# A down projection by seven products of eight, with its weight sums made in DRAM, in a transformer-block kernel on one core

## The chip, the core and the metric

The kernel runs on one core of a Trainium2 chip. Its engines are TensorE (PE, and PEld for its weight loads), VectorE (DVE), ScalarE (ACT), GpSimd (POOL) and SyncE (SP); SP and POOL issue the transfers, which all share 16 DMA engines. The metric is the device time of one execution in microseconds (us). 128x512 is 128 partitions by 512 fp32 elements.

## The reference, cut to what matters

```python
h = x + swa_mixer(rms_norm(x, attn_norm), ...)           # sliding-window attention, D_MODEL = 1024, SEQ = 1024
a = relu(rms_norm(h, mlp_norm) @ w_up)                   # 1024 -> 4096
h = h + (a * a) @ w_down                                 # 4096 -> 1024
h = rms_norm(h, final_norm)
# a second block of two layers follows: modulation vectors silu(c) @ w_mod (48 columns of 128), convolution, Fourier mixing,
# window attention; it isn't touched except that the 48 modulation rows are worked out in another place
```

## The kernel before

Activations are held transposed: features on partitions, the 1024 tokens along the free axis in two halves ("ti" 0 and 1, TN = 512). Every fp32 product is made of three matmuls (`mm3`): each operand is split into a high part (fp32r, cast by ACT) and a low part (the difference, made by DVE), and high x high, high x low and low x high are accumulated. So a 128x128 block of weights against 512 tokens costs PE three matmuls, and every operand costs ACT one copy and DVE one subtraction.

Each engine has a program written out in a fixed order; semaphores tie them. SP issues nearly all loads.

**Attention.** `mixed_attention` walks 16 steps k through a plan of slots, two slots a step (37 in all). Step k's scores are made in slots 2k and 2k+1, the exponentials in 2k+2. In slot 2k+3 DVE makes the denominators, then DVE normalises the even heads and POOL the odd ones (`divide`, L1115). PE transposes the normalised heads (L891, `turn`) in slots 2k+4 (tiles 0 and 1, even heads; the tile of odd heads as well where a step has two tiles only) and 2k+5 (tiles 2 and 3, odd heads, which need `divide`). PE's gaps between these are filled with the rest of the query projection and the output projection (`heads_pe`). POOL has nothing else to do here.

**Up projection.** Four of the 32 blocks of 128 hidden features are made directly. The other 28 go in 14 pairs by Strassen's scheme in Winograd's form over (2 halves of the features in) x (2 blocks out) x (2 halves of the tokens): seven products of 4 x 3 matmuls replace eight. The t-tiles (t1 to t4) are the sums of activations, the "forms" 0 to 6 of a pair are its weights or sums of weights: forms 0, 5 and 6 are plain, forms 1 to 4 sums. `form_sums` makes the sums on POOL (L1420 to L1428) from the pair's rows in `sraw`; ACT casts (`form_high`) and DVE subtracts (`form_low`) each form four products ahead (LEAD). The products accumulate in banks of PSUM; ACT copies a bank out between two products (`take`), DVE adds (`add_out`, L1861) and squares (L1866), and SP spills the hidden tile to DRAM.

**Down projection.** All plain: quarters of 8 hidden chunks, 24 units d of 48 matmuls and 16 jobs (`DOWN3`) of 24 matmuls, 1536 matmuls in all. Each unit loads 512 KB of weights and two rows of `mod_w`; DVE adds each result to `hm` (L1897, L1921), splits chunks (L1481) and weights (L168), and multiplies out the modulations (L1888, 96 of them, two a row of `mod_w`) between them.

Of the kernel before, what the change touches and what calls it, by code (L numbers as in the profile page):

```python
# [30 lines left out]
P = 128  # L31
# [16 lines left out]
STAGES = [("qkv", 10), ("wo", 8), ("mlp", 36), ("ein", 20), ("dft", 6), ("fw", 1), ("pw", 2),  # L48
# [6 lines left out]
UNITS = _n  # L55

# [43 lines left out]
def build(nc, t):  # L100
# [13 lines left out]
    with es:  # L114
# [451 lines left out]
        mH = [sb(f"mH{ti}", [KC, TN], A_R + 32 * ti * KB, F32R) for ti in range(2)]  # L566
        mL = [sb(f"mL{ti}", [KC, TN], A_R + (32 * ti + 16) * KB, F32R) for ti in range(2)]
# [164 lines left out]
        def mixed_attention(name, steps, X, pairs, t_tiles, chunks, heads, W, QH, QL, KH, KL, vzH, vzL, in1, sink_of, logits,  # L732
# [372 lines left out]
            def att_pool(pool):  # L1105
# [233 lines left out]
        def vec(ti):  # L1339
            return 1 if ti == 2 else 0  # L1340

        QUARTERS, MODS = 4, 3
        base = W0["mlp"]


        UP_DIRECT, PAIRS, FORMS, LEAD = 4, 14, 7, 4
        DOWN0, PRODUCTS = base + UP_DIRECT, PAIRS * FORMS
        V11, V21, V12, V22 = (lambda k: t1V[:, k, :]), (lambda k: t4V[:, k, :]), (lambda k: t3V[:, k, :]), (lambda k: t2V[:, k, :])
        t1V, t4V, t3V, t2V = (sb(f"t{n}V", [HALF, TN], A_R + at * KB) for n, at in ((1, 96), (4, 104), (3, 128), (2, 136)))
        t1L, t4L, t3L, t2L = (sb(f"t{n}L", [HALF, TN], A_R + at * KB, F32R) for n, at in ((1, 96), (4, 104), (3, 128), (2, 136)))  # L1350
        t1H, t4H, t3H, t2H = (sb(f"t{n}H", [HALF, TN], A_R + at * KB, F32R) for n, at in ((1, 112), (4, 120), (3, 144), (2, 152)))
        FORM_AT = [(A_WST + 12 * KB + 2 * KB * i, A_WST + 2 * KB * i) for i in range(6)] + \
                  [(A_R + 34 * KB, A_R + 32 * KB), (A_R + 38 * KB, A_R + 36 * KB)]
        formH = [sb(f"formH{i}", [TN], h, F32R) for i, (h, l) in enumerate(FORM_AT)]
        formL = [sb(f"formL{i}", [TN], l, F32R) for i, (h, l) in enumerate(FORM_AT)]
        formS = [sb(f"formS{i}", [TN], l) for i, (h, l) in enumerate(FORM_AT)]
        CHUNK_AT = [(48, 52), (0, 16), (4, 20), (40, 56), (44, 60), (8, 24), (12, 28), (32, 36)] + \
                   [(96 + 8 * i, 100 + 8 * i) for i in range(8)]
        chunkH = [sb(f"chunkH{i}", [SEQ], A_R + h * KB, F32R) for i, (h, l) in enumerate(CHUNK_AT)]
        chunkL = [sb(f"chunkL{i}", [SEQ], A_R + l * KB, F32R) for i, (h, l) in enumerate(CHUNK_AT)]  # L1360
        chunkR = [sb(f"chunkR{i}", [SEQ], A_R + l * KB) for i, (h, l) in enumerate(CHUNK_AT)]
        taken_out = sb("taken_out", [3, TN], RX)
        sraw = sb("sraw", [4, D], RX + 6 * KB)
        hid = sb("hid", [4, TN], RX + 22 * KB)
        mod_junk = sb("mod_junk", [D], RX, BF16)
# [1868 lines left out]
```

## Time and profile before

| | |
|---|---|
| median of 3 runs | 2095.6 us (2094.21 to 2097.47) |
| the profiled execution | 2095.91 us, of which the span of its trace is 2094.1 us (1.8 us lie around it) |
| PE busy | 96% of the span, 10014 matmuls |
| DVE, ACT, POOL busy | 65%, 39%, 15% |
| attention | about 100 to 300 us |
| up projection by products | about 389 to 656 us |
| down projection | about 656 to 1016 us |

Busy time of PE is read with care: matmuls overlap, so that the count of matmuls in a stretch tells more than the busy share.

### The profile page before, as it was taken

How to read it: one execution, taken by the hardware profiler on the slowest of the kernel's cores; microseconds unless marked ns; L12 is line 12 of the kernel's file. 1: busy time of each engine (PE TensorE's matmuls, PEld its weight loads, DVE VectorE, ACT ScalarE, POOL GpSimd, SP SyncE). 2: the span in 40 equal slices, each digit the busy share in tenths (PEclk: the TensorE clock that was granted, in tenths of full speed). 3: DMA queues.
4: the chain of work that ended last, by engine and by line, in shares of the span. 5: the costliest groups of instructions: out<-in, count | busy, mean ns of one | idle time of the engine just before them, and what ended most of it. 6: DMA issues, size and time to landing. Idle time of an engine off the chain costs nothing. (4 is left out here: it accounts for less than half of the span.)

```text
span 2094.1 us, 26033 instructions
## 1 busy us (share of the span) xinstructions
PE 2012.5 (96%) x10014; PEld 1658.0 (79%) x10014; DVE 1360.1 (65%) x2307; ACT 810.1 (39%) x1499; POOL 304.8 (15%) x262
## 2 busy tenths in 40 slices
PE   6999999999998999999999999989989999999997
PEld 4877787888887888888788888778877777888785
DVE  7278877655445877773689895774363456777644
ACT  4266544533334121213531232741242235555432
POOL 2023223222220000002400010000020012222200
PEclk9999999999999999999999999999999999999998
DMA  3202000423326555531231165234122211011212
GB/s 129 70 21 102 22 30 31 142 109 112 124 98 219 187 197 191 211 121 51 60 121 41 41 158 142 73 107 153 33 103 71 71 55 39 27 37 41 113 44 90
DMA packets 61562, 198.32 MB, mean 95 GB/s; under 512 B 7168, under 2 KB 11904, under 8 KB 60288
## 3 DMA queue, kind: packets, MB, share of 16 engines
q1 hardware_dynamic: 57408, 180.58, 24.9%
q0 software_dynamic: 1584, 7.29, 1.8%
q10 hardware_dynamic: 2448, 8.79, 1.1%
q8 instruction: 80, 1.31, 0.3%
q14 instruction: 42, 0.34, 0.1%
HBM read 152.64 MB, written 36.70 MB: 90 GB/s over the span
## 5 line engine op out<-in xcount | busy, mean ns | idle before, releaser
L173 PE MATMUL banks<-u2H,wH 128*128 128x512 f32 (+1 forms) x704 | 261.0, 371 | 4.6 <-POOL u2L L435 2.9
L174 PE MATMUL banks<-u2L,wH 128*128 128x512 f32 (+1 forms) x704 | 257.2, 365 | 0.0
L175 PE MATMUL banks<-u2H,wL 128*128 128x512 f32 (+1 forms) x704 | 256.9, 365 | 0.0
L163 ACT CAST wH<-raw 128x1024 fp32r<-128x1024 f32 x125 | 130.9, 1048 | 270.6 <-DMA raw<-in_wstream 268.5
L173 PE MATMUL banks<-chunkH,wH 128*128 128x512 f32 x512 | 201.4, 393 | 5.7 <-DVE chunkL L1481 5.6
L168 DVE TENSOR_TENSOR wL<-raw,wH 128x1024 fp32r<-128x1024 f32 x125 | 156.3, 1251 | 77.1 <-ACT wH L163 76.7
L174 PE MATMUL banks<-chunkL,wH 128*128 128x512 f32 x512 | 200.3, 391 | 0.0
L175 PE MATMUL banks<-chunkH,wL 128*128 128x512 f32 x512 | 200.1, 391 | 0.0
L1115 POOL TENSOR_SCALAR logits<-logits,stat 128x256 f32<-128x256 f32 (+3 forms) x96 | 121.2, 1275 | 341.0 <-DVE stat L990 341.0
L2205 DVE SCALAR_TENSOR_TENSOR conv_out<-conv_in,par,conv_out 128x1295 f32<-128x1295 f32 x108 | 162.7, 1566 | 0.6
L1888 DVE SCALAR_TENSOR_TENSOR mod_junk<-mod_w,cvec 128x1024 bf16<-128x1024 f32 x96 | 117.4, 1223 | 59.2 <-DMA mod_w<-in_mod_w 57.6
L173 PEld LDWEIGHTS banks<-u2H,wH 128*128 128x128 f32 x704 | 133.8, 190 | 27.7 <-issue 4.6
L175 PEld LDWEIGHTS banks<-u2H,wL 128*128 128x128 f32 x704 | 133.7, 190 | 21.3
L174 PEld LDWEIGHTS banks<-u2L,wH 128*128 128x128 f32 x704 | 133.9, 190 | 20.2 <-issue 0.2
L173 PEld LDWEIGHTS banks<-chunkH,wH 128*128 128x128 f32 x512 | 96.6, 189 | 27.8 <-DVE chunkL L1481 7.6
L175 PEld LDWEIGHTS banks<-chunkH,wL 128*128 128x128 f32 x512 | 96.7, 189 | 20.2
L174 PEld LDWEIGHTS banks<-chunkL,wH 128*128 128x128 f32 x512 | 96.7, 189 | 19.9 <-issue 0.2
L1084 ACT ACTIVATE logits<-logits,stat 128x256 f32<-128x256 f32 (+3 forms) x192 | 112.0, 586 | 0.0
L1452 DVE TENSOR_TENSOR formL<-sraw,formH 128x512 fp32r<-128x512 f32 x42 | 33.9, 808 | 98.1 <-ACT formH L1443 98.1
L173 PE MATMUL banks<-w2H,wH 128*128 128x512 f32 x208 | 88.3, 425 | 4.1 <-DVE wL L168 3.4
L174 PE MATMUL banks<-w2L,wH 128*128 128x512 f32 x208 | 83.0, 399 | 0.0
L175 PE MATMUL banks<-w2H,wL 128*128 128x512 f32 x208 | 82.7, 398 | 0.0
(387 smaller groups left out, 4717.9 us busy)
## 6 DMA issues: line engine op xcount, KB each, us to landing
raw<-in_wstream SPq DMA_DIRECT2D x125, 512.0 KB, 3.6
mod_w<-in_mod_w SPq DMA_DIRECT2D x48, 512.0 KB, 6.0
hidden_scratch<-hid SPq DMA_DIRECT2D x64, 256.0 KB, 2.0
chunkR<-hidden_scratch SPq DMA_DIRECT2D x32, 512.0 KB, 4.5
sraw<-in_sstream SPq DMA_DIRECT2D x28, 512.0 KB, 4.4
side_sum<-side_tap POOLq DMA_DIRECT2D x11, 647.5 KB, 5.8
gt<-gates_scratch SPq DMA_DIRECT2D x8, 640.0 KB, 3.9
h<-in_x SPq DMA_DIRECT2D x4, 1024.0 KB, 10.8
```

The costliest lines, as they stand in the source:

```text
L163: act.copy(wH[:, u % R, :], raw[:, u % R, :]).then_inc(weights_hi, 1)
L168: eng.tensor_tensor(wL[:, u % R, :], raw[:, u % R, :], wH[:, u % R, :].bitcast(F32), ALU.subtract)\
L173: first = pe.matmul(out, aH, bH, start=start, stop=False, skip_group_check=more)
L174: pe.matmul(out, aH, bL, start=False, stop=False, skip_group_check=more)
L175: return first, pe.matmul(out, aL, bH, start=False, stop=stop, skip_group_check=more)
L1084: m = act.activation(src, src, ACT.Exp, bias=stat[:, NEG, k % 3, hs:hs + 1], scale=0.125 / factor(steps[k]), accum_out=stat[:, SUM, k % 3, ...
L1115: m = pool.tensor_scalar(src, src, stat[:, SUM, k % 3, hs:hs + 1], None, ALU.mult)
L1452: dve.tensor_tensor(formL[form_slot(f)][:], form_source(f), formH[form_slot(f)][:].bitcast(F32), ALU.subtract)\
L1888: dve.scalar_tensor_tensor(mod_junk[:], mod_w[:, n % MODS, :], 1.0, cvec[:, v, :], ALU.mult, ALU.mult, accum_out=modv[:, n, v:v + 1]).then ...
L2205: dve.scalar_tensor_tensor(dst, src, w, dst, ALU.mult, ALU.add).then_inc(conv_step, 1)
```

## The change

- **Down projection.** 24 of the 32 hidden chunks, as 12 pairs kp (chunks kp and kp + 12), go by seven products. An output step handles two of the 8 output blocks and a span lo to hi of the pairs (`DOWN_WINDOWS`): 15 steps, whose spans are staggered so that at most five pairs are held at a time. Of each pair DVE makes four sums and seven low parts, ACT seven high parts (`prepare` says in which product's slot). DVE adds each product's bank to two or fewer tiles of `hm` (`down_add`) between one product and the next of the same bank. The last 8 chunks stay plain: the 16 jobs of `DOWN3`.
- **Weight sums.** `form_sums` and `sraw` go. The sums of all 29 steps (14 up, 15 down) are made in DRAM (`presum_step`): for each group of 4 steps, 1 MiB an array, four copies DRAM to DRAM and four accumulating transfers, in six parts, each part of which waits on POOL for the transfers of the part before. Two groups (lanes) take turns. The first 28 of the 48 parts are issued in the attention's slots 0 to 13, two a slot, after POOL's `divide`; the rest after POOL's work on the norm. SP then loads every form by itself (`form_load`, 256 KB or less) into a ring of ten.
- **Modulations.** 36 of the 48 rows are multiplied out during the up projection (three a pair), 12 during `DOWN3`.
- **Squares.** The squaring of the hidden tiles goes from DVE to ACT, as a ReLU and a square each.

The diff, cut to its core:

```diff
+DOWN_WINDOWS = [(0, 2), (0, 2), (0, 3), (0, 4), (2, 5), (2, 6), (3, 7), (4, 8), (5, 9), (6, 10), (7, 10), (8, 12),
+           (9, 12), (10, 12), (10, 12)]
...
-            def att_pool(pool):
+            def att_pool(pool, beside=None):
...
                 for i, slot in enumerate(plan):
                     if slot.sums:
                         divide(slot.k - 1)
...
+                    if beside:
+                        beside(pool, i)
...
+        def presum_step(pool, group, part):
+            lo, hi = PRESUM_GROUP * group, min(PRESUM_GROUP * group + PRESUM_GROUP, STEPS)
+            turn, count = presum[group % 2], 128 * (group // 2)
...
+            if part or group >= 2:
+                pool.wait_ge(turn, count + (PRESUM_DONE[part - 1] if part else 0))
+            if part == 0:
+                pool.dma_start(R1, A21).then_inc(turn, 16)
+                pool.dma_start(R3, A11).then_inc(turn, 16)
+            if part == 1:
+                pool.dma_start(R1, A22, accum_op=ALU.add, max_dma_last_dim=8192).then_inc(turn, 16)
+                pool.dma_start(R3, A21, accum_op=ALU.add, max_dma_last_dim=8192).then_inc(turn, 16)
+            if part == 2:
+                pool.dma_start(R2, R1).then_inc(turn, 16)
+            if part == 3:
+                pool.dma_start(R2, A11, accum_op=ALU.add, max_dma_last_dim=8192).then_inc(turn, 16)
+            if part == 4:
+                pool.dma_start(R4, R2).then_inc(turn, 16)
+            if part == 5:
+                pool.dma_start(R4, A12, accum_op=ALU.add, max_dma_last_dim=8192).then_inc(turn, 16)
+
+        GROUPS = (STEPS + PRESUM_GROUP - 1) // PRESUM_GROUP
+        PRESUMS = [(2 * pair + lane, part) for pair in range((GROUPS + 1) // 2) for part in range(PRESUM_STEPS)
+                   for lane in range(2) if 2 * pair + lane < GROUPS]
+        PRESUMS_BESIDE = 28
+
+        def presum_slot(pool, i):
+            for group, part in PRESUMS[2 * i:2 * i + 2] if 2 * i < PRESUMS_BESIDE else ():
+                presum_step(pool, group, part)
+
+        def form_load(sp, f):
+            n, i = divmod(f, FORMS)
...
+            elif f >= RING:
+                sp.wait_ge(forms_begun, f - RING + 2)
...
+            if i in SUMS:
+                group = n // PRESUM_GROUP
+                sp.wait_ge(presum[group % 2], 128 * (group // 2) + PRESUM_DONE[(1, 3, 5, 1)[SUMS[i]]])
+            source = sums_d[SUMS[i]][n] if i in SUMS else t["sblocks"][PLAIN[i]][n]
+            sp.dma_start(form(formR, f), source[:, 0:width(n)]).then_inc(form_loaded[f % 4], 16)
...
+        prepare(0, -1, 1, {0: (X11, X1), 1: (X2, X22), 2: (X3, X21), 3: (X4,)},
+                {0: (SUM1, SUM2, SUM3, SUM4), 1: (X11, X1), 2: (X2, X22, X3), 3: (X21, X4)})
+        prepare(1, -1, 5, {0: (X11, X1), 1: (X2, X22), 2: (X3, X21), 3: (X4,)},
+                {0: (SUM1, SUM2), 1: (SUM3, SUM4, X11), 2: (X1, X2), 3: (X22,), 4: (X3,), 5: (X21,), 6: (X4,)})
+        prepare(2, 0, 4, {1: (X11, X1), 2: (X2,), 3: (X22,), 4: (X3,), 5: (X21,), 6: (X4,)},
+                {0: (SUM1,), 1: (SUM2,), 2: (SUM3,), 3: (SUM4,), 4: (X11,), 5: (X1,), 6: (X2,), 7: (X22,), 8: (X3,), 9: (X21,), 10: (X4,)})
...
+        for n, kp in PREP.items():
+            prepare(kp, n, 2, {1: (X11, X1), 2: (X2, X22), 3: (X3, X21), 4: (X4,)},
+                    {0: (SUM1, SUM2), 1: (SUM3, SUM4), 2: (X11, X1), 3: (X2, X22), 4: (X3, X21), 5: (X4,)})
...
-            for q in range(PAIRS):
-                form_sums(pool, q)
-            pool.wait_ge(down_done, 48)
+            for group, part in PRESUMS[PRESUMS_BESIDE:]:
+                presum_step(pool, group, part)
+            pool.wait_ge(prod_done, PRODUCTS)
...
+            def down_add(s):
...
+                dst = hm[:, 2 * ((n - PAIRS) % 4) + row, TN * ti:TN * ti + TN]
+                dve.wait_ge(prod_done, s + 1)
...
+                dve.tensor_tensor(dst, dst, bank(out_bank(n, i)), op).then_inc(add_done, 1)
...
             for s in range(PRODUCTS):
+                n, i = divmod(s, FORMS)
+                if n < PAIRS and i >= 4:
+                    add_out(n, i - 4)
+                if s > UP_PRODUCTS:
+                    down_add(s - 1)
                 form_low(dve, s + LEAD)
+                if 0 < n <= MODS_UP // 3 and i in (0, 2, 5):
+                    modulations(3 * n - 3 + (0, 2, 5).index(i))
+                for kp, x in DVE_KP.get((n, i), ()):
+                    (kp_sum_of if x >= SUM1 else kp_low)(dve, kp, x)
...
             for j in range(14):
                 residual(j)
                 add(j)
+                if MODS_UP + j < 48:
+                    modulations(MODS_UP + j)
...
             @block.gpsimd
             def _(pool):
                 qkv_pool(pool)
-                swa_pool(pool)
+                swa_pool(pool, presum_slot)
```

## Rows read from the trace of the kernel before

**Rows 1.** The page: busy time of each engine, share of the span and instructions.

```profile
PE 2012.5 (96%) x10014; PEld 1658.0 (79%) x10014; DVE 1360.1 (65%) x2307; ACT 810.1 (39%) x1499; POOL 304.8 (15%) x262
```

**Rows 2.** Busy time by stretches: us, PE, PEld, DVE, ACT, POOL, PEclk, DMA share, GB/s.

```profile
110.00:180.00 70.00, 66.53 (x411) 52.79 (x410) 54.90 (x175) 43.18 (x136) 20.95 (x24) 1.00 0.08 24
400.00:500.00 100.00, 100.00 (x443) 82.83 (x442) 49.82 (x70) 36.08 (x62) 28.33 (x22) 1.00 0.30 112
700.00:800.00 100.00, 100.00 (x443) 82.85 (x442) 76.34 (x112) 19.05 (x19) 0.00 (x0) 1.00 0.52 196
```

**Rows 3.** The same view, where the up projection ends and the down projection begins.

```profile
655.00:660.00 5.00, 4.70 (x21) 3.55 (x19) 3.56 (x4) 0.00 (x0) 0.00 (x0) 1.00 0.51 145
660.00:665.00 5.00, 0.18 (x1) 0.18 (x2) 1.22 (x1) 2.50 (x4) 0.00 (x0) 0.93 0.97 324
665.00:670.00 5.00, 4.42 (x9) 2.60 (x10) 2.45 (x2) 3.88 (x4) 0.00 (x0) 0.50 0.93 327
670.00:675.00 5.00, 5.00 (x21) 4.02 (x21) 0.00 (x0) 3.41 (x3) 0.00 (x0) 0.89 0.97 399
```

**Rows 4.** POOL's timeline in the attention: start, us, instruction, idle before.

```profile
109.39 2.47 POOL L1115 TENSOR_SCALAR logits<-logits,stat 128x128 f32<-128x128 f32 x4 [60.11 <-DVE stat L990]
120.45 3.82 POOL L1115 TENSOR_SCALAR logits<-logits,stat 128x256 f32<-128x256 f32 x4 [8.59 <-DVE stat L990]
131.17 3.82 POOL L1115 TENSOR_SCALAR logits<-logits,stat 128x256 f32<-128x256 f32 x4 [6.90 <-DVE stat L990]
...
168.29 3.81 POOL L1115 TENSOR_SCALAR logits<-logits,stat 128x256 f32<-128x256 f32 x4 [8.25 <-DVE stat L990]
180.35 3.82 POOL L1115 TENSOR_SCALAR logits<-logits,stat 128x256 f32<-128x256 f32 x4 [8.25 <-DVE stat L990]
```

**Rows 5.** PE's timeline there: the turns of slots 7 and 15.

```profile
132.17 1.09 PE L891 MATMUL banks<-ident,logits 128*128 128x128 f32 x8
...
182.37 1.09 PE L891 MATMUL banks<-ident,logits 128*128 128x128 f32 x8
```

**Rows 6.** The page's DMA issues: engine, count, KB each, median us to landing.

```profile
side_sum<-side_tap POOLq DMA_DIRECT2D x11, 647.5 KB, 5.8
hm<-in_x SPq DMA_DIRECT2D x1, 4096.0 KB, 13.5
x_scratch<-x_out SPq DMA_DIRECT2D x2, 2048.0 KB, 7.4
xo<-x_scratch SPq DMA_DIRECT2D x1, 4096.0 KB, 12.7
```

**Rows 7.** DMA queues from 1205 to 1290 us: packets, MB, share of 16 engines.

```profile
q0 software_dynamic: 1584, 7.29, 43.5%
q1 hardware_dynamic: 864, 3.15, 15.2%
```

**Rows 8.** Groups of instructions on POOL: count, busy, mean ns, idle before.

```profile
L2160 POOL DMA_DIRECT2D side_sum<-side_tap x11 | 9.7, 880 | 207.5 <-ACT side_tap L2140 146.4 <-DMA side_sum<-side_tap 61.1
```

**Rows 9.** DVE's timeline in the up and in the down projection.

```profile
462.32 0.68 DVE L1866 SCALAR_TENSOR_TENSOR hid<-hid 128x512 f32<-128x512 f32 x1
462.93 0.68 DVE L1861 TENSOR_TENSOR hid<-banks,taken_out 128x512 f32<-128x512 f32 x1
...
760.20 1.23 DVE L1888 SCALAR_TENSOR_TENSOR mod_junk<-mod_w,cvec 128x1024 bf16<-128x1024 f32 x1 [5.93 <-DMA mod_w<-in_mod_w]
...
762.62 0.69 DVE L1897 TENSOR_TENSOR hm<-banks,hm 128x512 f32<-128x512 f32 x1
763.22 2.35 DVE L1481 TENSOR_TENSOR chunkL<-chunkR,chunkH 128x1024 fp32r<-128x1024 f32 x2
```

**Rows 10.** Who waited for whom: PE from 640 to 700 us.

```profile
PE banks L173 <- DVE chunkL L1481: 5.6, 2, 5.1
```

More of the change, by code:

```diff
@@ L1430, in form_source, with out_bank @@
[L1430 to L1432 removed]
+        W11, W12, W21, W22 = range(4)
+        PLAIN = {0: W11, 5: W12, 6: W22}
+        SUMS = {1: 0, 2: 1, 3: 2, 4: 3}
+        PRESUM_STEPS, PRESUM_GROUP = 6, 4
+        PRESUM_DONE = (32, 64, 80, 96, 112, 128)
+        def out_bank(n, i):
+            return ((2, 3, 4) if n and n % 2 == 0 else (7, 0, 1) if n % 2 else (4, 5, 6))[(0, 2, 0, 2, 0, 1, 0)[i]]
@@ new lines, in kp_freed, with kp_high @@
+        def kp_freed(eng, kp, i):
+            if kp >= KP_SLOTS:
+                if i == X4:
+                    eng.wait_ge(prod_done, step_done(LAST_USE[kp - KP_SLOTS]))
+            elif kp == 4:
+                for slot in range(4):
+                    eng.wait_ge(spilled[slot], 16 * (2 + PAIRS))
+                eng.wait_ge(prod_done, UP_PRODUCTS)
+            elif i != X11:
+                eng.wait_ge(prod_done, UP_PRODUCTS - FORMS + (1, 3, 5, 7)[kp])
+        def kp_high(act, kp, i):
+            if i in (X11, X21, X22):
+                hidden_loaded(act, 2 * kp + (i != X11))
+            else:
+                act.wait_ge(kp_sum, 4 * kp + {X1: 1, X2: 2, X3: 3, X4: 4}[i])
+            kp_freed(act, kp, i)
+            dst, src = kpH[kp % KP_SLOTS][i][:], kp_values(kp)[i]
+            if i == X2:
+                act.activation(dst, src, ACT.Copy, scale=-1.0).then_inc(kp_hi, 1)
+            else:
+                act.copy(dst, src).then_inc(kp_hi, 1)
@@ L3173, in layout @@
     units += [up[:4]]
-    for q in range(4):
-        units += [pack_units(down[D * q:D * q + D])]
+    units += [pack_units(down[3 * D:])]
     ein = pack_units(a["e_w_in_2"][0])
@@ L3203, in layout @@
     assert out["wstream"].shape == (UNITS, P, D), out["wstream"].shape
-    out["sstream"] = up[4:]
+    steps = np.zeros((4, len(DOWN_WINDOWS), P, 512), f)
+    for st, (lo, hi) in enumerate(DOWN_WINDOWS):
+        for row in range(2):
+            m = 2 * (st % 4) + row
+            for half in range(2):
+                block = down[P * (lo + 12 * half):P * (hi + 12 * half), P * m:P * m + P]
+                steps[2 * row + half, st, :, 0:P * (hi - lo)] = pack_units(block)[0]
+    first = up[4:].reshape(14, 2, P, 2, 512).transpose(1, 3, 0, 2, 4).reshape(4, 14, P, 512)
+    out["sblocks"] = np.concatenate([first, steps], 1)
     out["x"] = chunked(a["x"][0].T)
```

598 lines of the change are left out of this document (331 added, 267 removed).

## The prediction

> **What bounds the kernel now.** Read the page's first part first: PE is busy for 96% of the span [rows 1], and the other engines have room. The stretches by window then give PE's pace: 443 matmuls in 100 us at the full granted clock, in the up projection and in the down projection alike [rows 2], so one matmul is worth 100/443 = 0.2257 us. A change pays here by taking matmuls away or by closing gaps, and costs by opening gaps. The windows around 660 us show the one large gap of this part: 21, 1, 9 and 21 matmuls in four stretches of 5 us, where 22.2 fit in each [rows 3]. That is 88.6 - 52 = 36.6 matmuls, 8.3 us; the list of waits names it: PE waits for the low part of a hidden chunk [rows 10], which comes back from DRAM late. Of the 8.3 us some 2.5 are clock: the granted clock falls to 0.50 and 0.89 of full after PE's idle stretch [rows 3].
>
> **The matmuls taken away.** The spans of the 15 steps sum to 2+2+3+4+3+4+4+4+4+4+3+4+3+2+2 = 48 blocks. Each block is 7 products x 3 matmuls = 1008 matmuls, where the 24 plain units had 24 x 48 = 1152. So 144 go: -144 x 0.2257 = -32.5 us. `DOWN3` keeps its 384. The gap at 660 us goes too: the first pairs of chunks (0 with 12, 1 with 13) are in DRAM long before, and are prepared during the last up pair, on a DVE that has room for it. -8.3 us. At the new seam, before `DOWN3`, the eight chunks and two weight units are prepared two to three steps ahead, and I cost it at nothing.
>
> **DVE in the down projection.** One 128x512 operation follows another after 0.61 us (462.32 to 462.93), one of 1024 after 1.13 (2.35 less 1.22) [rows 9], so 0.52 us goes with each 512 columns: 0.35 us for a form of a span of 2, 0.48 for a span of 3. Over the whole stretch: 105 `down_add` x 0.61 = 64; forms 7 x (4 x 0.35 + 4 x 0.48 + 7 x 0.61) = 53; sums and low parts of the pairs 12 x 11 = 132, of which 16 lie in the last up pair, 116 x 0.61 = 71; chunks 8 x 1.13 = 9. Sum 197 us against 48 x 21 x 0.2257 = 227.5 us of PE. DVE is no bound on average, but a bank must be added out between two products, so it can't be averaged over steps. Steps 0 and 1 have 2 blocks (9.5 us of PE) and DVE work of 7 adds (4.3), 7 forms (2.5 to 3.0) and 9 and 8 operations of pairs 1 to 3 (5.5 and 4.9): 12.2 us each. PE waits 2.7 us in each: +5. If operations cost their full 0.69 us [rows 9] and each add also waits for PE, DVE's sum is 223 us, every step of 2 or 3 blocks is DVE's, and the cost is some +20; that it costs nothing is the other end.
>
> **The up projection.** A pair lasts 7 x 12 x 0.2257 = 19.0 us. DVE loses its squares and gains three rows of modulations, each 762.62 - 760.20 = 2.42 us [rows 9]: 7 forms and 3 adds x 0.61 + 7.3 = 13.4 us. The worst slot (a form, an add and a row) is 3.6 us against 2.7, made good in the next; forms are four products ahead. ACT, with the squares, stays under 12 us. Nothing. In `DOWN3` (5.4 us a job) an added row brings DVE to at most 4.8 us a job; the final small operations lie before the next norm: +1 us.
>
> **The weight sums beside attention.** This is what decides. POOL issues and *waits for* transfers in its own program, and behind each wait stands `divide`. Before, POOL idles 60 us before `divide` of step 0 (109.39), so parts 0 to 2 of the first two groups are covered. Then `divide` comes every 12 us, each with 7 to 9 us of idle time before it [rows 4]. Between the end of the first (111.9) and the seventh (180.35, slot 15) lie 68.5 us, and in slots 3 to 13 POOL issues: part 3 (2 accumulating), 4 (2 copies), 5 (2), 0 (4 copies), 1 (4), 2 (2 copies), 3 (2), 4 (2 copies), 5 (2), 0 (4 copies), and part 1 at the end. What must have landed before the seventh `divide` is 12 accumulating transfers and 14 copies of 1 MiB.
>
> Their price: a plain transfer of 2 MiB lands after 7.4 us and one of 4 MiB after 12.7 [rows 6], so 2.65 us per MiB and 2.1 us fixed. No row shows DRAM to DRAM; a copy uses the same 16 engines, and I take 2.65. The only accumulating transfers are those of `side_sum`, within SBUF: 7.29 MB = 6.95 MiB took 43.5% of 85 us = 37.0 us of all 16 engines [rows 7], 5.3 us per MiB. A transfer's issue costs POOL 0.88 us [rows 8].
>
> 12 x 5.3 + 14 x 2.65 = 100.7 us of transfers in 68.5 us. I walked it in order, a queue served first come first served: the next six `divide`s start at 126.4, 145.6, 176.5, 194.8, 214.0 and 224.6 us, the last 44 us late; 12 us of the 112.7 are issue and fixed time that nothing covers. The longest is 176.5 - 149.4 = 27.1 us, where eight transfers land in turn.
>
> Not all lateness reaches PE. The odd heads' turn comes two slots after: `divide` of slot 5 ends at 124.3 and its turn is at 132.17; that of slot 13 ends at 172.1, its turn is at 182.37 [rows 4, 5]. That is 10.3 us of slack at slot 13, whose `divide` is 214.0 - 168.3 = 45.7 us late: PE is pushed by 35 us. PE has no spare time to win this back [rows 2]. The other traffic holds 0.08 of the engines there [rows 2]; shared in packets it makes the chain some 10% longer: +43 instead of 35; I take +42. The clock falls in each wait as at 660 us, but only the last is not hidden behind POOL, +2; and the load of `hm` (13.5 us [rows 6]), wanted just after, shares the engines with the last four accumulating transfers, +2. Attention: +46 us.
>
> The bounds: if accumulating ran at a copy's 2.65 us per MiB, the ten rounds take 69 us and some 12 of latency, and PE loses under 10 us. If it costs twice the row in DRAM (10.6), the chain is 64 us longer: +105.
>
> **The sums after attention.** 9 copies and 9 accumulating MiB are left, 72 us of transfers, wanted from the 17th step on, 200 us later: the sums are in time. But SP's own loads share the engines: in 12 pairs (228 us) forms 21, spills 12 and modulations 18 MiB, 135 us. 207 of 228 us: it fits. If the queue of sums is served first, SP's loads fall back by at most 72 x 135/228 = 43 us, of which a form's lead of five products (13.5 us) covers part: 0 to +29, and I take +3.
> The Trainium skill (DMA: Bandwidth & Descriptors, "Queues, rings and completion order") says that a DMA engine goes round its queues and changes only after a whole packet; with long accumulating packets on the one side and short form packets on the other that rule would give nearer the upper end. The trace shows only that accumulating and other transfers share 1205 to 1290 us [rows 7], not what form loads would wait.
>
> **Sum.** 2095.9 (the profiled execution: span 2094.1 and 1.8 around it, 0.3 above the median of the runs) - 32.5 - 8.3 + 5 + 1 + 46 + 3 = 2110 us.
>
> **Rivals.**
> 1. *Attention isn't held up (ends faster).* POOL's idle time and PE's slack take the transfers in. For it: 6.9 to 8.6 us idle before each `divide`, up to 10.3 us of slack [rows 4, 5]. Against it: 100.7 us of transfers in 68.5 + 10.3. Without the push and its 4 us: 2064 us. It decides where attention's loss falls below 46 - 14 = 32 us, the push below 28: the transfers would have to take 97 us where I count 1.1 x 100.7 = 111, other traffic included; 3.7 us per MiB rather than 4.3. That is near; a whole absence is not.
> 2. *Accumulating in DRAM is much slower than in SBUF.* It reads two streams and writes one in DRAM. At twice the row: attention +105, total some 2170; at 1.3 times about 2130.
> 3. *Form loads starve in the up projection* (the packet rule above): +29 instead of +3, 2136.
> 4. *DVE bounds the down projection*: +20 instead of +5, 2125. If it eats all that seven products give, the change doesn't do what it is for.
>
> **Chances.** Forecast case, attention +30 to +60 with the rest as summed: 0.45 (2094 to 2126). Rival 1, a push under 30 us: 0.30. Rival 2: 0.13. Rivals 3 and 4 on top of the forecast: 0.12. A difference under 0.2% (4 us) can't be told from none. Faster: rival 1's most part and none else, 0.31. Same: the edges of rival 1 and of the forecast, 2091 to 2100, 0.12. Slower: the rest, 0.57. Range: from 2066 (rival 1 nearly whole) to 2150 (accumulating at 1.6 times the row), leaving out 0.2; the forecast case's own range is 2094 to 2126.
>
> **What would show it.** `divide` on POOL should start ever later against its sums' reciprocals, with POOL waiting for accumulating transfers, and PE's transposes L891 should wait for POOL several times between 140 and 230 us, 40 us in all; landing of an accumulating MiB tells the price. First product of the up projection: about 435 us instead of 389. From first up product to last job of `DOWN3`: some 595 us instead of 627. The windows should hold 443 matmuls in 100 us in the up projection, fewer in the first two output steps of the down projection, and no gap between up and down. I'm wrong if PE doesn't wait for POOL in the attention, if accumulating in DRAM isn't near 5.3 us per MiB, or if the products of the down projection run at DVE's pace.

## The result and the profile after

The changed kernel takes 2175.9 us (median of 4 runs, 2172.8 to 2178.8) against 2095.1 us (2094.2 to 2097.5): ratio 1.038 (1.0366 to 1.0394), 81 us slower. The forecast was 2110 with a range to 2150, so the sign was right and the time lies 26 us outside the range. The profiled execution took 2176.8 us, its span 2175.0.

The page of the changed kernel, against [rows 1]: busy time by engine; two of its DMA issues (count, KB each, median us to landing).

```profile
PE 1999.4 (92%) x9870; PEld 1640.2 (75%) x9870; DVE 1443.0 (66%) x2511; ACT 897.9 (41%) x1725; POOL 284.1 (13%) x270
...
sums_scratch<-in_sblocks POOLq DMA_DIRECT2D x28, 1024.0 KB, 11.5
...
hidden_scratch<-hid SPq DMA_DIRECT2D x64, 256.0 KB, 4.3
```

The 144 matmuls are gone (10014 to 9870), and PE fell from 96% to 92% of a longer span: what was lost is idle time of PE. To place it, compare four milestones, the first start of each kind of matmul (the tile views give them; before and after):

| stretch | before | after | difference |
|---|---|---|---|
| start to first product of the up projection | 389.1 | 460.1 | +71.0 |
| 98 products of the up projection | 267.0 | 302.1 | +35.1 |
| down projection before `DOWN3` (24 units; 15 steps) | 270.4 | 235.0 | -35.4 |
| `DOWN3` and the small operations up to the next norm's first product | 89.6 | 98.4 | +8.8 |
| the rest | 1078.0 | 1079.4 | +1.4 |

The sum is +80.9, the difference of the spans. PE's list of waits in the changed kernel (who waited for whom: us in total, times, longest) names the causes of the first two:

```profile
PE banks L893 <- POOL logits L1117: 53.6, 5, 20.7
PE banks L177 <- DVE wL L172: 24.6, 11, 9.1
PE banks L177 <- DVE hid L2038: 15.1, 1, 15.1
...
PE banks L177 <- ACT taken_out L1896: 9.2, 3, 4.9
```

**The attention.** POOL's timeline, to be read against [rows 4]. `divide` is L1117, copies are L1464, L1465, L1470 and L1474, accumulating transfers L1467, L1468, L1472 and L1476:

```profile
119.96 2.49 POOL L1117 TENSOR_SCALAR logits<-logits,stat 128x128 f32<-128x128 f32 x4 [27.95 <-DVE stat L992]
...
137.23 3.64 POOL L1117 TENSOR_SCALAR logits<-logits,stat 128x256 f32<-128x256 f32 x4
...
158.49 3.63 POOL L1117 TENSOR_SCALAR logits<-logits,stat 128x256 f32<-128x256 f32 x4
...
189.69 3.63 POOL L1117 TENSOR_SCALAR logits<-logits,stat 128x256 f32<-128x256 f32 x4
...
209.26 3.66 POOL L1117 TENSOR_SCALAR logits<-logits,stat 128x256 f32<-128x256 f32 x4
...
227.02 3.63 POOL L1117 TENSOR_SCALAR logits<-logits,stat 128x256 f32<-128x256 f32 x4
232.89 0.93 POOL L1467 DMA_DIRECT2D sums_scratch<-in_sblocks  x1 [2.24 <-DMA sums_scratch<-in_sblocks]
244.02 0.84 POOL L1468 DMA_DIRECT2D sums_scratch<-in_sblocks  x1 [10.20 <-issue]
244.56 1.14 POOL L1467 DMA_DIRECT2D sums_scratch<-in_sblocks  x1
258.82 0.81 POOL L1468 DMA_DIRECT2D sums_scratch<-in_sblocks  x1 [13.12 <-issue]
259.38 3.00 POOL L1117 TENSOR_SCALAR logits<-logits,stat 128x256 f32<-128x256 f32 x3
```

The seven `divide`s of slots 3 to 15 start at 120, 137, 158, 190, 209, 227 and 259, where they started 12 us apart before. From the second on nothing stands in the brackets: POOL goes into `divide` straight from issuing a transfer, and the idle time is in front of the transfers. The last interval is another kind. There is nothing to wait for by a semaphore, yet the second and the fourth of four accumulating transfers in a row stand 10.2 and 13.1 us before they are issued ("issue": no wait that the profile shows). It is not the only such place: of the two earlier rows of four, the fourth at 80 us stands 12.1 us, and the second and the fourth in slot 7 stand 5.3 and 8.6 us. What PE makes of it, its turn of slot 17:

```profile
263.42 1.94 PE L893 MATMUL banks<-ident,logits 128*128 128x128 f32 x8 [20.71 <-POOL logits L1117]
```

The same turn was at 193.59 before, so PE is pushed by 69.8 us, all but 1.2 us of what the first row of the table shows.

**The up projection.** DMA queues from 434 to 560 us (packets, MB, share of 16 engines; then issues, count, KB, median us to landing):

```profile
q0 software_dynamic: 1728, 18.88, 56.4%
q1 hardware_dynamic: 8803, 19.22, 42.7%
...
formR<-sums_scratch SPq DMA_DIRECT2D x20, 256.0 KB, 10.8
hidden_scratch<-hid SPq DMA_DIRECT2D x20, 256.0 KB, 10.8
```

The 16 engines are full (99%), and a 256 KB transfer lands after 10.8 us. From 400 to 500 us before, a spill of the same size took 2.0:

```profile
hidden_scratch<-hid SPq DMA_DIRECT2D x21, 256.0 KB, 2.0
```

By stretches of 10 us (us, PE, PEld, DVE, ACT, POOL, PEclk, DMA share, GB/s), where 44.3 matmuls would fit:

```profile
460.00:470.00 10.00, 7.19 (x26) 5.43 (x24) 4.35 (x4) 6.63 (x10) 1.70 (x2) 0.83 1.07 324
470.00:480.00 10.00, 5.07 (x14) 3.55 (x12) 2.73 (x3) 2.56 (x5) 1.23 (x3) 0.66 1.05 299
480.00:490.00 10.00, 5.70 (x18) 4.20 (x18) 2.02 (x4) 2.73 (x5) 3.50 (x6) 0.83 0.96 365
490.00:500.00 10.00, 4.68 (x21) 3.53 (x19) 0.66 (x2) 0.00 (x0) 0.55 (x1) 0.99 1.05 263
500.00:510.00 10.00, 0.18 (x1) 0.21 (x2) 1.29 (x2) 1.15 (x2) 1.03 (x2) 0.50 1.03 315
510.00:520.00 10.00, 10.00 (x37) 8.09 (x38) 4.15 (x7) 9.17 (x14) 1.64 (x2) 0.83 0.93 218
...
700.00:720.00 20.00, 20.00 (x89) 16.54 (x89) 14.79 (x24) 10.31 (x19) 0.00 (x0) 1.00 0.75 227
762.00:772.00 10.00, 9.19 (x39) 6.66 (x38) 9.80 (x20) 6.59 (x16) 0.00 (x0) 1.00 1.02 332
772.00:782.00 10.00, 9.70 (x41) 7.28 (x41) 10.00 (x20) 6.52 (x15) 0.00 (x0) 1.00 0.72 251
```

In the 60 us from 460 on PE made 117 matmuls instead of 266, which is 33.6 of the 35.1 us. Up to 510 us the DMA share is 0.96 or more and no other engine is busy for over 6.7 of 10 us. They wait for loads; who waited for whom from 455 to 520 us has ACT's longest wait, 18.4 us for a form:

```profile
ACT formH L1508 <- DMA formR<-sums_scratch: 20.8, 3, 18.4
```

Once the sums are done (700 to 720) the pace is that of [rows 2]. The last two rows are the first two steps of the down projection: 8.6 matmuls short of full, 1.9 us, with DVE at 98 to 100%.

**`DOWN3`.** Durations of the modulations' multiplications on DVE (ns min/median/max), and the timelines of POOL and DVE in one job:

```profile
L2031 DVE SCALAR_TENSOR_TENSOR mod_junk<-mod_w,cvec x24: 1218/1702/2194, 1004.8 to 1073.0; 128x1024 bf16<-128x1024 f32 x24
```

```profile
1016.73 2.32 POOL L1816 TENSOR_TENSOR g_acc<-g_acc,g_sq 128x512 f32<-128x512 f32 x1 [3.06 <-ACT g_sq L1943]
```

```profile
1016.68 1.22 DVE L2031 SCALAR_TENSOR_TENSOR mod_junk<-mod_w,cvec 128x1024 bf16<-128x1024 f32 x1
...
1017.94 2.19 DVE L2031 SCALAR_TENSOR_TENSOR mod_junk<-mod_w,cvec 128x1024 bf16<-128x1024 f32 x1
```

Two instructions of one shape take 1.22 and 2.19 us, and POOL's addition beside them 2.32 where it had 1.28 before (16 of them, 1276/1282/1295 ns).

### The profile page after: what moved, and what is told of

It is laid out like the page before. It is cut to its first block and busy times, and to the rows that moved or that the text cites. A ratio compares the mean times of both kernels' runs of the same rounds, so it can differ in the third digit from the quotient of the medians.

```text
span 2175.0 us, 26691 instructions
## 1 busy us (share of the span) xinstructions
PE 1999.4 (92%) x9870; PEld 1640.2 (75%) x9870; DVE 1443.0 (66%) x2511; ACT 897.9 (41%) x1725; POOL 284.1 (13%) x270
## 3 DMA queue, kind: packets, MB, share of 16 engines
q0 software_dynamic: 6832, 68.12, 12.4%
## 5 line engine op out<-in xcount | busy, mean ns | idle before, releaser
L1514 DVE TENSOR_TENSOR formL<-formR,formH 128x512 fp32r<-128x512 f32 (+2 forms) x203 | 128.2, 632 | 91.6 <-ACT formH L1508 91.3
L172 DVE TENSOR_TENSOR wL<-raw,wH 128x1024 fp32r<-128x1024 f32 x101 | 124.5, 1233 | 91.2 <-ACT wH L167 91.0
L1117 POOL TENSOR_SCALAR logits<-logits,stat 128x256 f32<-128x256 f32 (+3 forms) x96 | 120.3, 1284 | 252.3 <-DVE stat L992 252.1
L1508 ACT CAST formH<-formR 128x512 fp32r<-128x512 f32 (+2 forms) x203 | 112.6, 572 | 72.7 <-DMA formR<-in_sblocks 48.1
L177 PE MATMUL banks<-kpH,formH 128*128 128x512 f32 x336 | 131.7, 392 | 3.8 <-DVE hm L2051 3.0
L179 PE MATMUL banks<-kpH,formL 128*128 128x512 f32 x336 | 130.8, 389 | 0.0
L178 PE MATMUL banks<-kpL,formH 128*128 128x512 f32 x336 | 130.8, 389 | 0.0
L893 PE MATMUL banks<-ident,logits 128*128 128x128 f32 x544 | 81.0, 294 | 53.6 <-POOL logits L1117 53.6
L893 PEld LDWEIGHTS banks<-ident,logits 128*128 128x128 f32 x544 | 63.6, 149 | 66.1 <-issue 60.5
L2031 DVE SCALAR_TENSOR_TENSOR banks<-mod_w,cvec 128x1024 f32<-128x1024 f32 x72 | 88.6, 1230 | 7.4 <-DMA mod_w<-in_mod_w 6.1
L2051 DVE TENSOR_TENSOR hm<-hm,banks 128x512 f32<-128x512 f32 x105 | 72.0, 686 | 30.9 <-PE banks L179 30.3
```

The lines of the kernel that those rows point to most:

```text
L172: eng.tensor_tensor(wL[:, u % R, :], raw[:, u % R, :], wH[:, u % R, :].bitcast(F32), ALU.subtract)\
L177: first = pe.matmul(out, aH, bH, start=start, stop=False, skip_group_check=more)
L178: pe.matmul(out, aH, bL, start=False, stop=False, skip_group_check=more)
L179: return first, pe.matmul(out, aL, bH, start=False, stop=stop, skip_group_check=more)
L893: m = pe.transpose(banks[:, T_BANK + g % T_RING, j * P:j * P + P], logits[:, k % 3, hs, off:off + P], ident[:])
L1117: m = pool.tensor_scalar(src, src, stat[:, SUM, k % 3, hs:hs + 1], None, ALU.mult)
```

## The experiments

The kernel before was run beside each group: 2093.7 us (the first four), 2095.3 (the next four), 2095.9 (the last three).

**No sums at all.** Are both losses the sums' or does something else of the change (the ring of forms, the modulations, the squares on ACT) slow the up projection? Forms 1 to 4 are loaded from plain blocks and no sum is made, so the weights of those products are not the scheme's.

```diff
-            for group, part in PRESUMS[2 * i:2 * i + 2] if 2 * i < PRESUMS_BESIDE else ():
-                presum_step(pool, group, part)
+            pass
...
-            if i in SUMS:
...
-            source = sums_d[SUMS[i]][n] if i in SUMS else t["sblocks"][PLAIN[i]][n]
+            source = t["sblocks"][SUMS[i] if i in SUMS else PLAIN[i]][n]
...
-            for group, part in PRESUMS[PRESUMS_BESIDE:]:
-                presum_step(pool, group, part)
```

> The changed kernel without any sum made in DRAM: forms 1 to 4 are loaded from the plain blocks in place of their sums (so what is left out is the making of the weight sums; every load, cast, product and addition stays). Theory (the sums' transfers cost twice: POOL's waits beside attention and unit loads delayed before it, 71 us, and SP's loads held up behind them in the up projection, 35 us): first up product back at 389 us, 98 up products in 267 us, total 2176 - 71 - 35 = 2070 us. Rival (the ring of ten forms with SP's many loads is too slow by itself, whatever POOL does): the up projection stays at about 300 us and the total is near 2105.

2067.8 us, ratio 0.987 (0.981 to 0.994). First product at 387.1 us, the 98 products take 266.5 us (267.0 before). So attention's and the up projection's losses are wholly the sums'. And it's not the amount of SP's own traffic. Its queues from 434 to 560 us:

```profile
q1 hardware_dynamic: 13116, 28.98, 75.1%
...
formR<-in_sblocks SPq DMA_DIRECT2D x47, 256.0 KB, 2.9
...
hidden_scratch<-hid SPq DMA_DIRECT2D x26, 256.0 KB, 3.3
```

The forms, spills and modulations alone keep the engines busy for 75% of the time there, and form loads still land after 2.9 us.

**Only 12 of 48 parts beside the attention.** These are all six parts of the first two groups, in slots 0 to 5; parts 0 to 2 are those that [rows 4] let me cost at nothing. 42 MiB of sums are left for the time after the attention, instead of 18.

```diff
-        PRESUMS_BESIDE = 28
+        PRESUMS_BESIDE = 12
```

> Only the first 12 of the 48 parts beside attention (PRESUMS_BESIDE = 12), the other 36 after it. Theory (POOL's waits hold attention up by what is issued in slots 6 to 13): PE no longer waits for POOL's divide, first up product at about 400 us (the 11 us lost before the first divide stay). In the up projection 42 MiB of sums are left instead of 18, so if SP's loads starve in proportion, the 35 us grow to some 80: total 2176 - 60 + 45 = 2161. Rival (the starving is a thing of the first transfers only): total 2176 - 60 = 2116.

2190.8 us, 1.046 (1.040 to 1.052). PE no longer waits for `divide`, and the first product comes at 408.3 us: still 19 us after the kernel before. Of these, 9 us stem from the parts in slots 0 to 5: the first `divide` is at 119.44, and the last is 9.2 us late (293.97 for 284.77). The other 10 us come later, when POOL issues the next sums from 373 us on, and PE waits up to 7.2 us for `wL` in front of the first product. The 98 products take 367.8 us, +101, and the waits are those of late transfers:

```profile
PE banks L177 <- DVE hid L2038: 51.4, 5, 36.5
PE banks L177 <- DVE wL L172: 31.6, 12, 8.8
PE banks L177 <- ACT taken_out L1896: 21.3, 6, 5.0
```

Moving sums from the attention to the up projection only moves the loss.

**Copies in place of accumulating transfers.** The same bytes land, but no addition is made, so the sums are missing from the weights. It is meant to tell the accumulation's share from that of the mere traffic. The edit also drops the 8 KB limit on these transfers' packets, so the copies in their place go in long packets.

```diff
-                pool.dma_start(R1, A22, accum_op=ALU.add, max_dma_last_dim=8192).then_inc(turn, 16)
+                pool.dma_start(R1, A22).then_inc(turn, 16)
```

(and likewise the other three)

> Every accumulating transfer is a plain copy to the same place (so the sums are wrong, they are the last operand alone); waits, sizes and order stay. Theory of the prediction (an accumulating MiB costs twice a copy's): the chain of 26 MiB beside attention shrinks from some 137 to 80 us, PE waits for divide under 15 us in place of 54; the up projection loses some 15 instead of 35: total about 2176 - 45 - 20 = 2111. Rival (POOL's waits cost a fixed time each, whatever the transfer does): total within 15 us of 2176.

2134.7 us, 1.019 (1.012 to 1.027). PE's wait for POOL falls from 53.6 to 12.4 us and the first product comes 27.1 us sooner, the up projection is 12.0 us shorter. So without the additions about half of the loss goes, and half stays with the copies. What remains before the first product (+43.9) is in good part not a wait for POOL (the first `divide` is even later, 123.40). The two effects aren't apart here, since the edit lengthens packets as well; a later experiment (copies in packets of 8 KB) shows what long packets cost.

```profile
PE banks L177 <- DVE wL L172: 27.4, 12, 10.9
PE banks L177 <- DVE pT1L L972: 16.7, 5, 7.4
...
PE banks L893 <- POOL logits L1117: 12.4, 3, 7.5
```

Its software queue from 110 to 275 us, 30 MiB of copies only, gives the price of a copy in DRAM: 0.534 x 165 / 30 = 2.94 us per MiB.

```profile
q0 software_dynamic: 960, 31.46, 53.4%
```

**Sums paced.** Slots 0 to 2 as in the change, then one part every second slot, the last 26 parts behind the attention, one for four products.

```diff
+            if i < 3:
+                steps = PRESUMS[2 * i:2 * i + 2]
+            else:
+                steps = PRESUMS[6 + (i - 4) // 2:7 + (i - 4) // 2] if i % 2 == 0 and i <= 34 else ()
...
+            for x, (group, part) in enumerate(PRESUMS[PRESUMS_BESIDE:]):
+                if x >= 2:
+                    pool.wait_ge(prod_done, 4 * (x - 1))
                 presum_step(pool, group, part)
```

> The same transfers spread out: six parts in slots 0 to 2 as before, then one part of one group every second slot up to slot 34, the last 24 in the up projection one for every 4 products. Theory: a wait on POOL finds its transfer landed, so attention loses only the 11 us before the first divide; in the up projection a burst is 1 to 2 MiB, less than a form's lead, so it loses under 10 us: total 2070 + 11 + 10 = 2091. Rival (SP's loads lose by the total amount of the sums' traffic, not by its bursts): the up projection keeps its 35 us, total 2116.

2115.5 us, 1.010 (1.004 to 1.016). First product at 410.7, 98 products in 286.2. The wait for `divide` is gone; left are the early stretch (PE's longest wait for `wL` 9.2 us) and one stall of 15.0 us some 50 us into the up projection, where sums and loads still collide (from 440 to 480 us a form from the sums lands after 23.4 us).

**Late start.** The same 28 parts, two a slot, but from slot 3 on. If the first `divide` is 10.6 us late because of the early parts, it comes back on time.

```diff
-            for group, part in PRESUMS[2 * i:2 * i + 2] if 2 * i < PRESUMS_BESIDE else ():
+            for group, part in PRESUMS[2 * i - 6:2 * i - 4] if 0 <= 2 * i - 6 < PRESUMS_BESIDE else ():
```

> The 28 parts beside attention begin in slot 3 in place of slot 0 (slots 3 to 16). Theory (the first divide is 11 us late because the weight loads of the query projection share the DMA engines with parts 0 to 2): PE's wait of 9 us for weights before 110 us goes and the first divide is back at 109.4 us; but 6 copies and 4 accumulating MiB, 37 us of transfers, are no longer covered and come on top of POOL's chain: attention loses some 60 + 37 us, total 2176 - 11 + 37 = 2202. Rival (parts 0 to 2 cost nothing where they are, the 11 us are something else of the change): first divide stays at 120 us.

```profile
109.01 2.49 POOL L1117 TENSOR_SCALAR logits<-logits,stat 128x128 f32<-128x128 f32 x4 [60.11 <-DVE stat L992]
```

It does (before 109.39, changed 119.96). The total is 2191.9 us, 1.047 (1.044 to 1.049), since all of the chain then stands in `divide`'s way: PE waits 76.4 us for it.

**Copies in packets of 8 KB.** The changed kernel's four kinds of copies carry no limit on a packet; the queue's counts show what that does. From 49 to 110 us its software queue moved the same 10.49 MB in 768 packets (13.7 KB on average) as this experiment's 1440 (7.3 KB). The rival: the engines' time is what counts, whatever its grain.

```diff
-                pool.dma_start(R1, A21).then_inc(turn, 16)
-                pool.dma_start(R3, A11).then_inc(turn, 16)
+                pool.dma_start(R1, A21, max_dma_last_dim=8192).then_inc(turn, 16)
+                pool.dma_start(R3, A11, max_dma_last_dim=8192).then_inc(turn, 16)
```

(and likewise R2 and R4)

> The copies between DRAM buffers go in packets of 8192 bytes like the accumulating transfers, in place of 65536. Theory A (a packet of 65536 bytes holds a DMA engine 2.4 us, and SP's loads of the forms stand behind it): SP's loads land sooner while the copies run, the 98 up products take 285 in place of 302 us, and the first divide is less late; POOL's waits in attention, set by the bytes, stay near 54 us. Total near 2155. Theory B (SP's loads lose by the bytes that the sums move, not by the packet): no change, 2176 +- 5.

```profile
q0 software_dynamic: 1440, 10.49, 61.5%
...
raw<-in_wstream SPq DMA_DIRECT2D x6, 512.0 KB, 9.3
```

```profile
109.87 2.49 POOL L1117 TENSOR_SCALAR logits<-logits,stat 128x128 f32<-128x128 f32 x4 [16.93 <-DVE stat L992]
```

2154.4 us, 1.029 (1.027 to 1.031): 21.5 us less than the change. The first `divide` is on time again though the same bytes take the same share of the engines (61.5% against 60.8%), so it was the long packets; the median landing of SP's weight loads falls only from 10.9 to 9.3 us, but PE's longest wait for `wL` from 9.1 to 3.2. PE's wait for POOL, 52.2 us, is as before: the chain in the attention isn't a matter of packets of copies. The up projection takes 294.1 us, 8 less than the change, where I had expected 17 less: the long packets are a quarter of that loss. Shorter packets also cost something at the issue. POOL now stands before copies too, which it never does in the changed kernel, and before accumulating transfers 55.4 us for 49.9:

```profile
POOL sums_scratch L1465 <- issue: 11.1, 2, 5.8
```

**Paced and spread to the end of the attention.** Slots 0 to 2 with each part tied to the progress of the projections on PE, one part every second slot, four at the end, and the last 22 behind every seventh product.

```diff
+            if i < 3:
+                for x in (2 * i, 2 * i + 1):
+                    pool.wait_ge(qkv_done, 2 * x + 2)
+                    presum_step(pool, *PRESUMS[x])
+            elif i % 2 == 0 and i <= 34:
+                presum_step(pool, *PRESUMS[6 + (i - 4) // 2])
+            elif i == 36:
+                for x in range(22, 26):
+                    presum_step(pool, *PRESUMS[x])
...
+                pool.wait_ge(prod_done, 7 * (x + 1))
                 presum_step(pool, group, part)
```

> Spread wider than the last spread version: parts 0 to 2 of the first two groups one for every two jobs of the query projection, then one every second slot, four in POOL's idle time after attention, the last 22 one for every 7 products, into the down projection. Theory: no burst is over 2 MiB and none follows another at once, so SP's loads keep up: first up product at 392 us or less, up products 270 us, total 2068 + 5 = 2073. Rival (it is the amount of traffic): up products 280 us and more, total over 2085.

2100.7 us (8 runs), 1.003 (1.002 to 1.005), 28 us above the expectation. The first product comes at 407.6, 18.5 us after the kernel before (expected: 392 or less); pacing by the query projection didn't help, the first `divide` is at 120.88. The up projection takes 275.0 us, +8. And 8 of the last 22 parts (5 of 22 MiB) now lie beside the 15 steps of the down projection, which take 241.6 us for 235.0 in the change.

**The same with packets of 8 KB**, and with the low parts of the split ahead of the modulations in `DOWN3` (the rival for that stage: not the order but the durations are at fault).

```diff
+                pool.dma_start(R1, A21, max_dma_last_dim=8192).then_inc(turn, 16)
...
-                if MODS_UP + j < 48:
-                    modulations(MODS_UP + j)
                 if down3_split(j):
                     split_lo(dve, DOWN0 + down3_split(j))
+                if MODS_UP + j < 48:
+                    modulations(MODS_UP + j)
```

> The same spread, the copies in packets of 8192 bytes, and in the 16 last jobs DVE splits the next weights before it multiplies out a row of modulations, not after. Theory: the last 16 jobs took 98.4 us where 16 x 24 x 0.2257 = 86.7 would do, because the weights' low part stands behind the modulations (PE waits 8.5 us for it); they take 90 us now, total 2073 - 8 = 2065. Rival (DVE hasn't the time for both, its order doesn't matter): 98 us again.

2081.6 us, 0.994 (0.993 to 0.996): 0.6% faster than the kernel before. First product at 390.9 (before: 389.1), up projection 274.0 us, `DOWN3` 97.2 us. The order in `DOWN3` was worth 1 us of its 9; DVE's 24 multiplications still take 35.0 us there, 1460 ns on average. In the up projection a form load lands after 6.2 us from 400 to 500 us, and PE gets 437 of 443 matmuls there.

**26 parts beside the attention.** Moves the four accumulating transfers at which POOL stands from 232 to 259 us behind the attention.

```diff
-        PRESUMS_BESIDE = 28
+        PRESUMS_BESIDE = 26
```

> PRESUMS_BESIDE = 26 in place of 28: only part 1 of the third pair of groups (four accumulating MiB, issued in slot 13) moves behind attention. In the prediction's walk that part cost POOL 4 issues of 0.88 us, since nothing in attention waits for its landing. Theory (the trace of the changed kernel has POOL idle 10.2 and 13.1 us between two issues of accumulating transfers there, with no semaphore behind it: an issue has to wait until earlier accumulating transfers are done): attention gets 20 to 25 us back, first up product near 438 us; the four MiB come back in the up projection at 5 to 8 us; total 2176 - 22 + 6 = 2160. Rival (the walk of the prediction): under 4 us, total 2176 or more.

2168.0 us, 1.035 (1.032 to 1.038). PE's wait for POOL falls from 53.6 to 30.3 us and the first product comes 17.2 us sooner (442.9); 9.5 us of it are given back in the up projection (311.6), to which these 4 MiB go.

**A short addition on POOL in `DOWN3`**, on top of the kernel that is paced and has packets of 8 KB. `g_acc` adds 8 of 512 columns, so the sum of squares of the norm behind it is incomplete.

```diff
-                pool.tensor_tensor(g_acc[:, ti, :], g_acc[:, ti, :], g_sq[:, j % 2, :], ALU.add)
+                pool.tensor_tensor(g_acc[:, ti, 0:8], g_acc[:, ti, 0:8], g_sq[:, j % 2, 0:8], ALU.add)
```

> The last timed version, but POOL's 16 additions for the final norm's gain sum (g_acc) go over 8 columns in place of 512 (what is left out is that sum). Theory (a row of modulations on DVE and POOL's addition, both with two operands in SBUF, stretch each other: 2.19 in place of 1.22 us, 2.32 in place of 1.28): rows take 1.22 us again and the 16 last jobs 89 us in place of 97; total 2075 - 8 = 2067 beside the last version's profiled 2075. Rival (DVE simply has too much in these jobs): 97 us as before.

```profile
L2039 DVE SCALAR_TENSOR_TENSOR mod_junk<-mod_w,cvec x24: 1215/1222/1227, 917.4 to 978.6; 128x1024 bf16<-128x1024 f32 x24
```

2078.7 us, 0.993 (0.990 to 0.995). DVE's 24 multiplications all take 1.22 us, `DOWN3` 89.8 us (97.2 without the edit, 89.6 before the change).

**`cvec` in PSUM**, the same base, everything computed. ACT writes silu(c) of the second part into four banks that are free by then, and DVE reads it there.

```diff
+        cvec_p = banks[:, 0:4, :].rearrange("p (v a) f -> p v (a f)", v=2)
...
-            act.activation(cvec[1][:], cvec[1][:], ACT.Silu).then_inc(consts_set, 1)
+            act.wait_ge(add_done, FORMS * len(DOWN_WINDOWS))
+            act.activation(cvec_p[:], cvec[1][:], ACT.Silu).then_inc(consts_set, 1)
...
-                    ... 1.0, cvec[part][:, v, :], ALU.mult, ALU.mult,
+                    ... 1.0, (cvec_p if part else cvec[0])[:, v, :], ALU.mult, ALU.mult,
```

> The last timed version with silu(c) in banks 0 to 3 of PSUM for the 12 rows of modulations in the last 16 jobs, so that DVE reads one operand from SBUF and one from PSUM; POOL's additions whole. Theory (the stretching comes from DVE's second operand in SBUF): rows take 1.22 us, the 16 jobs 89 us, total near 2067. Rival 1 (any DVE operation beside POOL is stretched): 97 us. Rival 2 (DVE has too much in these jobs): rows at 1.22 us, but 95 us and more.

```profile
L2041 DVE SCALAR_TENSOR_TENSOR mod_junk<-mod_w,banks x24: 1205/1218/1222, 920.5 to 982.6; 128x1024 bf16<-128x1024 f32 x24
```

2078.0 us (4 runs, 2074.1 to 2080.6), 0.992 (0.989 to 0.994). All 24 at 1.22 us, 29.2 us together for 35.0, which is 5.8 of the 6.7 us that `DOWN3` gains (97.2 to 90.5). POOL's additions are at 1273/1292/1300 ns. It is 18 us faster than the kernel before and 98 faster than the change. Against the version without the edit the median fell by 3.5 us only, not 6.7, and the runs of the two overlap (2075.7 to 2083.5 there), so the gain is read from `DOWN3` and not from the total: the up projection took 279.8 us in this run's profile where it had taken 274.0, with no edit there.

## Why the prediction was wrong, step by step

| term | predicted | measured |
|---|---|---|
| products of the down projection, gap at 660, first steps | -32.5 - 8.3 + 5 = -35.8 | -35.4 |
| attention, first `divide` (costed at nothing) | 0 | +10.6 |
| attention, the rest | +46 | +60.4 |
| up projection | +3 | +35.1 |
| `DOWN3` tail | +1 | +8.8 |
| rest | 0 | +1.4 |

The misses, 10.6 + 14.4 + 32.1 + 7.8 + 1.4 + 0.4 = 66.7 us, on 2110 give 2176.7, the profiled 2176.8.

**The down projection** was right in its sum and in the main terms; that it agrees within 0.4 us is partly luck. The trace has 1008 matmuls there and no gap between up and down. The 15 steps take 235.0 us, 7.5 more than 1008 matmuls at full pace (227.5). But the first two steps lose 1.9 us where I had 5, and the rest is lost later, some 1.7 us of it from 984 to 990 us (19 matmuls, where 26.6 fit), near the last two steps, where I had nothing. Rival 4 (DVE bounds it) is out: PE's waits for `hm` are 3.0 us in all.

**The attention's mechanism was right**, rival 1 (no delay) was not, nor was rival 2: POOL stands before transfers, `divide` comes late, and PE waits for it. The walk holds up to the sixth `divide`: from the end of the first to the start of the sixth I had 214.0 - 111.9 = 102.1 us, the trace has 227.02 - 122.45 = 104.6. The prices held too, together. From 110 to 275 us the software queue's row is

```profile
q0 software_dynamic: 2752, 31.46, 75.1%
```

31.46 MB are 30 MiB, 14 copies and 16 accumulating transfers: 0.751 x 165 / 30 = 4.13 us per MiB; the two prices that I took (2.65 and 5.3) give (14 x 2.65 + 16 x 5.3) / 30 = 4.06. With the 2.94 of a copy from the experiment with copies alone, accumulating comes out at (123.9 - 14 x 2.94) / 16 = 5.2 us per MiB, by estimate: the copy was priced a little low, accumulating about right.

**Step that failed: the issue of a transfer at 0.88 us.** For the last `divide` I added 4 issues and walked on, 214.0 to 224.6, as though POOL could leave any number of transfers behind it. The trace has 227.0 to 259.4, 22 us more. POOL's waits for itself:

```profile
POOL sums_scratch L1468 <- issue: 49.9, 6, 13.1
```

The experiment with 26 parts takes away just these four and brings back 17.2 us. That the issue, and not a landing, holds POOL is read from the trace, where no wait of the program stands at that place, and from this experiment. It may not be a matter of adding: with copies in packets of 8 KB POOL stands before copies too, and with copies in long packets alone it stands for 3.5 us in all. That points to the number of packets under way, but no edit shows it by itself. So: 22 of the 69.8 us of push; with 2.5 of the walk and 10.6 of the late start it makes the push of 35 into 70, and my 11 us of allowances (other traffic, clock, `hm`) were not needed: 10.6 + 35 + 22 + 2.5 = 70.1.

**Step that failed: parts 0 to 2 "are covered".** I looked only at POOL's 60 us of idle time. But the six loads of weights by SP lie in the same stretch, landing after 10.9 us instead of 3.5, and with them comes a wait of PE for `wL` of 9.1 us. The late start and the 8 KB packets each bring the first `divide` back (109.0, 109.9); the second does it with the traffic unchanged, which shows that the length of the packets did it. In the two paced kernels with long packets the first product was 21.6 and 18.5 us late, and with 8 KB packets 1.8 (390.9).

**Term that was mis-sized: the up projection, +3 for +35.** Rival 3 had the mechanism and +29, with a chance that it shared with rival 4 of 0.12. My sum of the time of transfers, 207 of 228 us, was itself low: in the kernel without sums, SP's queue over 228 us (405 to 633) has

```profile
q1 hardware_dynamic: 23877, 52.25, 73.6%
```

which is 168 us of the engines for 49.8 MiB, 3.4 us per MiB where I took 2.65 (135 us in all). With my 72 us of sums that makes 240 of 228. And the sum was no argument: the sums of weights aren't spread over the 228 us but stand at its beginning, where the engines are at 99% and a load takes 10.8 us for 2.0, and PE has its 33.6 us of loss in the first 60. With no sums at all the loss is nothing, with 42 MiB instead of 18 it is +101, paced it is +8. The rule that I weighed there (the Trainium skill, DMA: Bandwidth & Descriptors, "Queues, rings and completion order": an engine goes on to the next queue after a whole packet) agrees with the 8 KB packets, which bring it from +35 to +27; but most of the loss isn't the length of packets but that there's no pace.

**Term that was mis-sized: `DOWN3`, +1 for +8.8.** I priced an added row at 2.42 us from [rows 9], a stretch in which POOL is idle. In `DOWN3` POOL adds squares, and one of each row's two multiplications takes 2.19 us for 1.22. Rearranging DVE didn't help (97.2 us); shortening POOL's addition (89.8) or moving one operand of DVE to PSUM (90.5) each did. Those two are shown by edits on either side. The Trainium skill (SBUF — State Buffer, "Who interferes with whom") says that a DVE instruction with two SBUF inputs contends with a GpSimd instruction that reads SBUF; the traces agree, 1.22 to 2.19 us on the one side and 1.28 to 2.32 on the other.

**A slip in the chances.** "Faster" had 0.31 as the most part of rival 1, which had only 0.30 in all.

**Left open.** How much can be under way before an issue stands, and whether transfers, bytes or packets count there. Shorter packets for the accumulating transfers weren't tried. What the sums beside the 15 steps cost in the paced kernels (237.9 to 241.6 us for 235.0) wasn't tested by itself. Why the up projection keeps 7 to 13 us of loss in the three best kernels, and why it differs between them (274.0 to 279.8), isn't settled; in the paced kernel with packets of 8 KB the 16 engines are 91% busy over the whole of it, which may be why. In the fastest the spans differ from before by +2.1 (up to the first product), +12.8 (up projection), -30.9 (15 steps), +0.9 (`DOWN3`) and -0.3 (rest), -15.4 us in all: half of what the seven products give is still eaten.

## What to carry to other kernels

Background transfers have three prices, and the sum of bytes shows none of them: what their issue does to the engine that issues, what they do to the landing of every other load in the same stretch, and where they stand in time. So give them a pace tied to the consumer's progress and packets short enough for the neighbours' loads (with an eye on the issues, which stood longer with short packets here), and take the cover of each stretch from the queues as well as from the engine. An operation's duration from one stretch holds in another only if the same neighbours are busy there.

## What the runs showed of the hardware

- Accumulating transfers in DRAM cost the engines about as much as those within SBUF: 5.2 us per MiB by the estimate above, against 5.3 in [rows 7]; a copy in DRAM cost 2.94. But of four in a row, 1 MiB each, the second and the fourth were issued 10.2 and 13.1 us late, and GpSimd stood for that time.
- With copies in packets of 8 KB GpSimd stood before two copies as well (11.1 us); in the changed kernel, whose copies go in long packets, before none.
- Copies DRAM to DRAM without a limit on the packet held the loads of another queue: with 8 KB packets the first `divide` came 10.1 us sooner at the same bytes.
- 1024-column DVE operations on two SBUF operands and POOL additions on SBUF stretch each other by 80%; with one of DVE's operands in PSUM neither is stretched.
- The granted clock fell where PE waited. From 180 to 300 us the granted clock was 0.81, where it was 1.00 before:

```profile
180.00:300.00 120.00, 76.46 (x436) 61.34 (x437) 56.05 (x178) 42.03 (x137) 38.69 (x49) 0.81 0.72 202
```
